# A gate table of one 256-column fp32r product per token, with the weighted rows made on DVE and all keys found before the stage

## The reference, cut to what matters

```python
q = (xt @ w_q).reshape(T, H, 2, PEER_DKEY // 2)
s = jnp.einsum('thcd,hcnd->thcn', q, sub_keys)
top_s, top_i = lax.top_k(s, K)
cand = (top_s[:, :, 0, :, None] + top_s[:, :, 1, None, :]).reshape(T, H, K * K)
best_s, best_j = lax.top_k(cand, K)
expert = jnp.take_along_axis(cand_i, best_j, axis=-1)
g = jax.nn.softmax(best_s, axis=-1)
act = jax.nn.gelu(jnp.einsum('cd,chkd->chk', xc, u_tab[ec]), approximate=False)
out = jnp.einsum('chk,chkd->cd', gc * act, v_tab[ec])
```

## Time and profile before

| | |
|---|---|
| median of three runs | 3056.68 us |
| span of the profiled execution | 3061.3 us (its own time is this span; it lies 4.6 us above the median of the runs) |
| busy in the span | PE 2891.4 (94%), weight loads 2353.4 (77%), DVE 1468.3 (48%), POOL 1399.4 (46%), ACT 996.5 (33%) |
| mean granted clock of TensorE | 0.962 of 2.4 GHz |
| chain that ended last | PE 78%, DVE 7%, issue 7%, POOL 5%, ACT 3% |
| the stage | 1597 to 2076 us |

### The profile page before, as it was taken

The page is one execution under the profiler, slowest core; times in us unless marked ns, Lnnn a source line. Parts: engine busy times, 40 slices in busy tenths (PEclk is TensorE's granted clock), DMA queues, the critical chain, the costliest instruction groups (busy, mean ns, idle before and its releaser), DMA issues.

```text
span 3061.3 us, 35543 instructions
## 1 busy us (share of the span) xinstructions
PE 2891.4 (94%) x13610; PEld 2353.4 (77%) x13610; DVE 1468.3 (48%) x2341; ACT 996.5 (33%) x1463; POOL 1399.4 (46%) x553
## 2 busy tenths in 40 slices
PE   7988899998989999888989999999999999999997
PEld 5745787876876678667878888888888888888886
DVE  3376421222145523447968779550003555555554
ACT  3255321222134532333233333332223222222222
POOL 5691454544320023433346777774445444444441
PEclk9979999998987999999999999999999999999999
DMA  3200222323210012322234556556455666666652
GB/s 126 69 0 30 80 92 88 108 74 148 83 56 1 1 55 82 110 83 69 90 124 149 167 158 195 186 158 196 146 200 169 192 193 193 194 193 194 193 193 70
DMA packets 222318, 375.89 MB, mean 123 GB/s; under 512 B 11152, under 2 KB 142608, under 8 KB 211216
## 3 DMA queue, kind: packets, MB, share of 16 engines
q1 hardware_dynamic: 222224, 374.68, 37.4%
HBM read 305.43 MB, written 69.21 MB: 122 GB/s over the span
## 4 chain that ended last, share of the span: by engine, by line
PE 78%; DVE 7%; issue 7%; POOL 5%; ACT 3%; DMA 0%; POOLq 0%; SPq 0%; DVEq 0%; ACTq 0%
PE bank L255 15%; PE bank L256 15%; PE bank L257 15%; PE bank L1835 8%; PE bank L1836 8%; PE bank L1837 8%; POOL rows_b L1651 4%; DVE cacc L434 2%; PE bank L1167 2%; PE bank L1138 2%; PE bank L1815 1%; PE bank L1147 1%; POOL u_lo L1615 1%; DVE xl L398 1%; PE bank L1757 0%
## 5 line engine op out<-in xcount | busy, mean ns | idle before, releaser
L247 POOL TENSOR_TENSOR w_lo<-w_raw,w_hi 128x2048 fp32r<-128x2048 f32 (+2 forms) x96 | 419.1, 4366 | 757.2 <-ACT w_hi L242 757.0
L1632 POOL TENSOR_TENSOR v_lo<-v_raw,v_hi 128x1024 fp32r<-128x1024 f32 x128 | 308.5, 2410 | 376.9 <-ACT v_hi L1628 376.9
L1615 POOL TENSOR_TENSOR u_lo<-u_raw,u_hi 128x1024 fp32r<-128x1024 f32 x128 | 324.6, 2537 | 340.1 <-ACT u_hi L1609 340.1
L2002 DVE TENSOR_TENSOR h_lo<-h_raw,h_hi 128x512 fp32r<-128x512 f32 x128 | 309.9, 2421 | 351.2 <-ACT h_hi L1637 351.1
L255 PE MATMUL bank<-xh,w_lo 128*128 128x512 f32 x1056 | 422.6, 400 | 34.8 <-DVE xl L398 17.8
L256 PE MATMUL bank<-xl,w_hi 128*128 128x512 f32 x1056 | 417.9, 396 | 0.0
L257 PE MATMUL bank<-xh,w_hi 128*128 128x512 f32 x1056 | 417.4, 395 | 0.0
L255 PE MATMUL bank<-xh,u_lo 128*128 128x512 f32 x1024 | 405.0, 395 | 0.3 <-POOL u_lo L1615 0.3
L1835 PE MATMUL bank<-h_hi,v_lo 128*128 128x512 f32 x1024 | 399.5, 390 | 4.2 <-DVE h_lo L2002 4.2
L256 PE MATMUL bank<-xl,u_hi 128*128 128x512 f32 x1024 | 399.5, 390 | 0.0
L257 PE MATMUL bank<-xh,u_hi 128*128 128x512 f32 x1024 | 399.4, 390 | 0.0
(11 more groups left out here) (339 smaller groups left out, 4471.6 us busy)
## 6 DMA issues: line engine op xcount, KB each, us to landing
w_raw<-w_small SPq DMA_DIRECT2D x80, 1024.0 KB, 4.9
u_raw<-expert_u SPq DMA_DIRECT2D x128, 512.0 KB, 3.7
v_raw<-expert_v SPq DMA_DIRECT2D x128, 512.0 KB, 5.1
h_scratch<-h_act SPq DMA_DIRECT2D x128, 256.0 KB, 2.1
g_scratch<-stage SPq DMA_DIRECT2D x8, 4096.0 KB, 16.8
h_raw<-h_scratch SPq DMA_DIRECT2D x128, 256.0 KB, 2.7
g_in<-g_scratch SPq DMA_DIRECT2D x64, 512.0 KB, 4.1
w_raw<-w_small SPq DMA_DIRECT2D x8, 768.0 KB, 4.3
```

The source lines that it names most:

```text
L247: pool.tensor_tensor(wl[g % 2][:, :n], raw[g % 2][:, :n], wh[g % 2][:, :n].bitcast(F32), ALU.subtract).then_inc(sem("lo_done"), 1)
L1615: pool.tensor_tensor(u_lo[c % 2][:, :, :], u_raw[c % 4][:, :, :], u_hi[c % 2][:, :, :].bitcast(F32), ALU.subtract)\
L1632: pool.tensor_tensor(v_lo[c % 4][:, :], v_raw[c % 4][:, :], v_hi[c % 4][:, :].bitcast(F32), ALU.subtract)\
L2002: dve.tensor_tensor(h_lo[c % 4][:, :], h_raw[c % 4][:, :], h_hi[c % 4][:, :].bitcast(F32), ALU.subtract)\
```

## The change

- The table matmul is fp32r. `rows_b` holds for each token two halves side by side, the one-hot key times the weight's high part and times its low part, and one matmul of 256 columns per token multiplies both by `rows_a`. A bank then holds two tokens, each with a high and a low table; a batch fills four banks instead of two.
- `rows_b` is written by DVE with one `tensor_scalar` per token and half: compare `iota_key` (0 to 127) with the token's key, times the token's weight. That is 16 instructions of 128 elements per batch, with two operands that are a value per partition. `hits` is gone.
- `rows_a` is written by POOL with one `tensor_scalar` per token (8 per batch of 128 elements, one compare).
- ACT copies the low table of each bank to `stage` (4 copies of 256 elements per batch), and DVE adds the high table to it (`stage_rows`, 4 additions of 256), which frees the bank.
- All keys are found ahead of the stage: `PRE` is 32 instead of 16 (so `POST` is 32 instead of 48), the exponential comes behind gelu of chunk 10, and the transposes of tiles 0 to 3 behind chunks 16, 20, 24 and 28. POOL's `row_keys(0)` still stands behind all low halves up to chunk PRE + 1.

```diff
-        hits = [at(f"hits{i}", [P, BT, NK], o, BF16) for i, o in enumerate((scr(25), WL + 14 * KB))]
-        rows_a = [at(f"rows_a{i}", [P, BT, NK], scr(8 + 4 * i)) for i in range(2)]
-        rows_b = [at(f"rows_b{i}", [P, BT, NK], o) for i, o in enumerate((WL + 10 * KB, CONST + 9 * KB))]
+        rows_a = [at(f"rows_a{i}", [P, BT, NK], scr(8 + 4 * i), F32R) for i in range(2)]
+        rows_b = [at(f"rows_b{i}", [P, BT, 2, NK], o, F32R) for i, o in enumerate((WL + 8 * KB, scr(0)))]
...
-        PRE = 16
+        PRE = 32
+        EXP_AT = 10
+        TURN_AT = (16, 20, 24, 28)
...
+            def row_keys(n):
+
+                if n >= 2:
+                    pool.wait_ge(sem("g_done"), 4 * n + 4)
+                for t in range(BT):
+                    ins = pool.tensor_scalar(rows_a[n % 2][:, t, :], iota_key[:, :], key_row[:, BT * n + t:BT * n + t + 1],
+                                             None, ALU.is_equal)
+                ins.then_inc(sem("a_rows"), 1)
+
+            wait(pool, ("pk_idx", 1 + QT))
+            row_keys(0)
+            row_keys(1)
+            for n in range(NBATCH):
+                if n + 2 < NBATCH:
+                    row_keys(n + 2)
+                split_u_lo(pool, 0, PRE + n + 2)
...
+                    for g in range(4):
+                        act.wait_ge(sem("g_done"), i * BG + (4 * n + g + 9))
+                        t = n % 8 * BT + 2 * g
+                        low = lin_bank[g][:, :].rearrange("p (t h c) -> p h c t", t=2, h=2)[:, 1]
+                        act.activation(stage[q][:, :, t:t + 2], low, ACT.Copy).then_inc(sem("g_low"), 1)
...
-                        for t in range(4):
-                            a, b = rows_a[n % 2][:, g % 2 * 4 + t, :], rows_b[n % 2][:, g % 2 * 4 + t, :]
-                            done = pe.matmul(lin_bank[g % 4][:, t * P:(t + 1) * P], a, b, start=True, stop=True)
+                        for t in range(2):
+                            a, b = rows_a[n % 2][:, g % 4 * 2 + t, :], rows_b[n % 2][:, g % 4 * 2 + t, :, :]
+                            done = pe.matmul(lin_bank[g % 4][:, t * 2 * NK:(t + 1) * 2 * NK], a,
+                                             b.rearrange("p h c -> p (h c)"), start=True, stop=True)
...
+            def weight_rows(n):
+
                 if n >= 2:
+                    dve.wait_ge(sem("g_done"), 4 * n + 4)
+                for t in range(BT):
+                    token = slice(BT * n + t, BT * n + t + 1)
+                    for half, w in enumerate((weight_hi[:, token].bitcast(F32), weight_lo[:, token])):
+                        ins = dve.tensor_scalar(rows_b[n % 2][:, t, half, :], iota_key[:, :], key_col[:, token], w,
+                                                ALU.is_equal, ALU.mult)
+                ins.then_inc(sem("b_rows"), 1)
+
+            def stage_rows(n):
+
+                q = n // 8 % 2
+                for g in range(4):
+                    dve.wait_ge(sem("g_low"), 4 * n + g + 1)
+                    t = n % 8 * BT + 2 * g
+                    out = stage[q][:, :, t:t + 2]
+                    high = lin_bank[g][:, :].rearrange("p (t h c) -> p h c t", t=2, h=2)[:, 0]
+                    dve.tensor_tensor(out, high, out, ALU.add).then_inc(sem("g_free"), 1)
...
+            for tt in range(QT):
+                places(tt)
+                mark_places()
+                keys(tt)
+            weights_low(QT - 1)
+            dve.wait_ge(sem("pk_low"), QT)
+            weight_rows(0)
+            weight_rows(1)
+            for n in range(NBATCH):
+                stage_rows(n)
+                if n + 2 < NBATCH:
+                    weight_rows(n + 2)
```

More of the change, by code:

```diff
@@ L1519, in peer_credits @@
         def peer_credits(pool):
[L1521 removed]
+            for name, n in (("pk_s", 4), ("pk_sc", 4), ("g_done", 8), ("g_free", 4), ("pk_t", 1), ("pk_idx", 1),
                             ("g_stored0", 16), ("g_stored1", 16), ("a_rows", 4), ("b_rows", 4),
@@ L1693, in block3_act @@
                 gelu(act, 0, c)
[L1694 to L1704, removed]
+                if c == EXP_AT:
+                    act.wait_ge(sem("pk_gsub"), 1)
+                    act.activation(best_e[:, :, :, :], best_e[:, :, :, :], ACT.Exp).then_inc(sem("pk_gexp"), 1)
+                if c in TURN_AT:
+                    turned(TURN_AT.index(c))
+            with act.Fori(0, QT) as i:
                 for n in range(NB8):
-                    if n == TURN_AT and not last:
-                        turn(i + 1)
                     q = n // 8
[L1709 to L1717, removed]
+                    if n % 8 == 0:
+                        act.wait_ge(sem(f"g_stored{q}"), i * 16 + 16)
+                    for g in range(4):
[3 more added lines that the diff above has]
+                        act.activation(stage[q][:, :, t:t + 2], low, ACT.Copy).then_inc(sem("g_low"), 1)
                     split_u_hi(act, i, PRE + n + 2)
                     gelu(act, i, PRE + n)
[L1721 to L1724, removed]
             for c in range(PRE + MID, NK):
@@ L1788, in block3_pe @@
                 activations(0, c)
-            for c in range(2, PRE):
-                activations(0, c)
-            pe.wait_ge(sem("bank_free"), 4 + TILES_AFTER[-1])
             def turn(i):
                 pe.wait_ge(sem("pk_keys"), i + 1)
-                pe.wait_ge(sem("pk_idx"), i + 1)
+                wait(pe, ("pk_idx", 1 + i), ("pk_low", i))
                 for j in range(3):
@@ L1801, in turn @@
                 last.then_inc(sem("pk_t"), 1)
-            def token_rows(i, last):
+            for c in range(2, PRE):
+                activations(0, c)
+                if c in TURN_AT:
+                    turn(TURN_AT.index(c))
+            pe.wait_ge(sem("bank_free"), 4 + TILES_AFTER[-1])
+            with pe.Fori(0, QT) as i:
                 for n in range(NB8):
-                    if n == TURN_AT and not last:
-                        turn(i + 1)
                     pe.wait_ge(sem("a_rows"), i * NB8 + (n + 5))
                     pe.wait_ge(sem("b_rows"), i * NB8 + (n + 5))
-                    for g in (2 * n, 2 * n + 1):
+                    for g in range(4 * n, 4 * n + 4):
                         pe.wait_ge(sem("g_free"), i * BG + (g + 1))
-                        for t in range(4):
-                            a, b = rows_a[n % 2][:, g % 2 * 4 + t, :], rows_b[n % 2][:, g % 2 * 4 + t, :]
-                            done = pe.matmul(lin_bank[g % 4][:, t * P:(t + 1) * P], a, b, start=True, stop=True)
+                        for t in range(2):
+                            a, b = rows_a[n % 2][:, g % 4 * 2 + t, :], rows_b[n % 2][:, g % 4 * 2 + t, :, :]
+                            done = pe.matmul(lin_bank[g % 4][:, t * 2 * NK:(t + 1) * 2 * NK], a,
+                                             b.rearrange("p h c -> p (h c)"), start=True, stop=True)
                         done.then_inc(sem("g_done"), 1)
                     activations(i, PRE + n)
-            turn(0)
-            with pe.Fori(0, QT - 1) as i:
-                token_rows(i, False)
-            token_rows(QT - 1, True)
             with pe.Fori(QT, QT + POST // MID_STEP) as i:
```

51 lines of the change are left out of this document (20 added, 31 removed).

## The result

The changed kernel takes 3027.57 us (median of 4 runs, 3024.62 to 3029.14) against 3057.52 us (4 runs) for the kernel before, taken on the same chip: a ratio of 0.990, with an interval of 0.9887 to 0.9915. So it is 1% faster, where the prediction had it 0.5% slower. The spans of the profiled executions are 3061.3 and 3027.4 us, 33.9 us apart.

The account below looks back on a forecast made before the run. PE bounds the kernel before; after the change DVE, held up by POOL, was to set the beat. 3061.3 + 16 (stage) - 4 (its start) + 3 (key search) = 3076, 3072 on the median's scale; range 2988 to 3142.

Parts of the forecast that it names:

- the price of POOL's compare: POOL, per batch: eight one-operation compares of 128 elements at 0.46 us each, 3.7 us (2.1 at the other end).
- the second rival: In the stage: port shared well but POOL the bound, beat 7.2 us, 3041 us (3005 to 3050); chance 14%.
- DVE's rows: DVE, per batch: sixteen `tensor_scalar` of 128 elements at 0.25 us, 4.0 us; four additions 1.45 us more.
- T + 1.23: Start of POOL's low half, 1.23 us after a batch's matmuls start at T; it runs until T + 3.62.
- the forecast's mechanism: In the stage: POOL's low half holds DVE's rows, PE waits for `b_rows`, beat 7.62, taken as 7.7 us; chance 46%.
- Token matmuls: PE, per batch: eight 256-column fp32r matmuls 0.12 us apart, 0.96 us; with the chunk's 5.46, PE alone allows 6.42.
- b = 1.2 us: DVE, per batch: time its rows lose to POOL's compares at the shared port, a third of 3.7 us.
- Whole instructions do not exclude each other: Denies the third rival: DVE and POOL instructions exclude each other entirely, 10.1 us per beat, 3224 us; chance 15% (3142 and more).
- The start of the stage: Ahead of the first token matmul: PE waits about 7.3 us in place of 11.7, -4 us.
- The key search: Tiles 1 to 3 moved to the chunks ahead of the stage: DVE's 4.42 us instructions delay low halves, +3 us.
- The stage: The 63 beats between token batches: 7.7 us each in place of 7.44, +16 us.
- The check list: Signs expected in the profile after: matmul spacing, beat, PE released by `rows_b` not `rows_a`, DVE and POOL instruction times.

## Why the prediction was wrong

*The step that failed* is the price of POOL's compare. The prediction took 0.46 us each, 3.7 per batch, scaled from a one-operation line and with 0.26 as the other end. It is 0.578, 4.62 per batch, above both ends. POOL therefore has 7.0 us and not 6.1, and is the bound: the second rival, with 14%, whose beat was put at 7.2 and whose time at 3041 (3005 to 3050). That rival named the right engine, but by another sum: 2.39 + 3.7 + 1.1 for DVE's rows in POOL's way, where it is 2.38 + 4.62 and nothing for the rows.

*What rested on it.* The forecast placed the low half behind ACT's high half, at T + 1.23, and added: "This stays so." It stays so only while POOL has room. With 7.0 us of work POOL runs late by 4.6 us and the low half lies beside the additions. Where POOL does have room, the forecast's mechanism is what happens. It had DVE held by the low half, PE waiting for it, and a beat of 7.62 to 7.7. With half of the compares the mean is 7.5, with seven 7.6, and both kernels are slower than the one before, as the forecast had it. That the size fits as well is in part luck. The forecast had the first row held for 2.17 - 1.2 = 0.97 us and 5.2 us of rows behind it; with half of the compares the row stands for 2.24 (2072.00 to 2074.24) and the other 15 take 4.13 (to 2078.37). What it took for its case was the case of a cheaper instruction.

*Token matmuls* 0.12 apart and PE's own beat of 6.42: right, and seen in the first batches. *DVE's rows*: 0.256 us apart where nothing disturbs them, for 0.25; the additions 1.40 for 1.45. *What the engines share*: b = 1.2 us was too much. In the changed kernel 15 rows take 4.38 us beside the compares (2035.07 to 2039.45) where alone they take 3.84: 0.5 us. The other direction is nothing in the changed kernel (0.578 with DVE busy or idle), but it was 0.07 us per compare with the low half on DVE (0.645). Whole instructions do not exclude each other here: two rows fit beside one compare of 0.578. They do for a long subtraction on POOL against `tensor_scalar` on DVE, as the earlier trace rows had shown.

*The start of the stage*: 8.3 us for 7.3 forecast, all of the difference again the compares. *The key search*: some 4 us for +3, of which 2.0 are the wait behind DVE's 4.42 us that the prediction had named, and 1.3 the four transposes. *The stage*: -30.6 us for +16.

*The check list* would have told the cases apart only in part. It expected PE to be released by `rows_b` or `rows_a`. The release came from `u_lo`, which stands on POOL behind the compares: the wait shows where the queue ends, not what fills it.

## What to carry to other kernels

Price an instruction on GpSimd by the same operation at the same size, or measure it: scaled from one of 512 elements, the compare came out at 0.46 us for 0.578, and this error of 0.12 us, eight times per batch, decided which engine was the bound. Where two engines hold each other up, a long instruction of the one should lie beside work of the other that does not wait for it (here: additions with an operand in PSUM), or move to the engine where it is short. The second cost 17 us by itself, and brought 25 only together with a row moved the other way and the four additions made one: it takes a new balance of both engines. And taking work off the bounding engine is not sure to gain: if its lateness has kept two instructions apart, the room that it wins lets them meet.

## What the runs showed of the hardware

- POOL's `tensor_scalar` of 128 fp32 elements: 0.578 us with one operation, 0.695 with two, one behind the other, the same with DVE idle or busy with `tensor_scalar` in these two kernels. With the low half moved to DVE the first is 0.645. One with 1024 elements as `tensor_tensor` (a subtraction with repeated operands) takes 1.9 us, so eight short ones cost more than twice one long one.
- A POOL `tensor_tensor` holds a DVE `tensor_scalar` to its end (up to 2.5 us for one of 0.33) but not an addition with an operand in PSUM. A DVE `scalar_tensor_tensor` with two operands in SBUF holds POOL's compares: 0.73 us each in place of 0.578. DVE's low half, a `tensor_tensor` of 1.14 us with two operands in SBUF, holds one of them for up to 1.84.
- DVE has a record for the time in which it is held, so the windows count it as busy.
